# A gated unit in seven half products: first token sum, operand slots and the order of its preparation changed

## The chip, the cores and the metric

The kernel runs on one core of a Trainium2 chip. The metric is device time of one execution in microseconds. Three runs of the kernel before took 1392.05, 1392.38 and 1394.17 us; the median is 1392.38 us.

## The reference, cut to what matters

One step of a two-layer decoder for 512 prompt tokens and 8 sample tokens (520 columns here). The first layer is a state space mixer with a gated unit; the second is dilated attention. The change lies in the gated unit:

```
ga, gb = split(gelu(y) @ w_glu + b_glu, 2)   # y: 520 x 2048, w_glu: 2048 x 4096
y = ga * sigmoid(gb) * silu(z)               # 520 x 2048
out = y @ w_out                              # 2048 x 1024
```

## The kernel before, in words

Activations lie transposed: 128 features on the partitions, 520 tokens along a row. Every fp32 matrix product is made of three matmuls on rounded operands: each operand is split into a high part (rounded to fp32r on ScalarE, ACT) and a rest (operand minus high part), and the terms are high x high, high x rest, rest x high. So each weight block needs a load into `raw`, a `w_hi` on ACT and a `w_lo` on GpSimd (POOL) or VectorE (DVE) before TensorE (PE) can multiply it.

The kernel is a row of blocks of code, each with one list of instructions for each engine; at a block's border all engines wait for each other. The change touches the blocks `outputs` (it ends with the GELU), `glu` and the start of `residual` for `a_out`. The order of the work in a block is that in which each engine's function is written; engines meet through semaphores.

**The end of `outputs`.** ScalarE writes `act_hi`, VectorE `act_lo` (L1303). PE turns the last rows and then runs tile 0 of the gated unit early (`early_tile`). A tile is 128 output features over all 16 feature blocks; it has two units of 8 blocks (1024 x 128 weights), 48 matmuls each. Units 0 to 7 are the "plain" or standard units: they make output tiles 0 and 1 in the ordinary way (gb and ga of each). They use two `raw` buffers and two operand slots by turns; slot n % 2 is free for unit n when unit n-2 has been multiplied. GpSimd makes their rest (`split_lo`, L111); SP loads unit n into `raw` when the rest of unit n-2 is made.

**The groups.** The other 14 output tiles are made by seven half products each in place of eight: a 2 x 2 block scheme over halves of the features and halves of the tokens (260 columns), in the manner of Strassen and Winograd. It needs four sums of tokens (t1 to t4, each again high and rest, made once) and, in each group, four sums of weight blocks (`sum_weights(g, i)`, i = 0 to 3: gb1+gb2, that minus ga1, ga1-gb1, and ga2 minus the second; L1691 to L1697, into PSUM). Product p of a group (24 matmuls, L1542) takes raw weights for p = 0, 1, 6 (rest by GpSimd's `raw_lo`, L1488) and summed weights for p = 2 to 5 (rest by VectorE's `sum_lo`, L1703). There are three operand slots for the products; slot n % 3 (by a list) is free when product n-3 has been multiplied.

**Token sums.** t1, t2, t3 are made in nine chunks on VectorE: `first_sum` (L1668, the difference, two SBUF inputs, into PSUM), high part on ACT (L1560), then `low_sum` (L1675 to L1679, three dependent ops). They start with the block `glu`. t4 (`last_sum`, two halves c = 0, 1 of four steps each: L1470, ACT's rounding L1565, L1475, L1479, L1481) is made on GpSimd. PE waits for t1 at product 3, t2 at product 2, t3 at product 4, t4 at product 6 of the first group.

**Gates.** ACT moves each product or its running sum out of PSUM (`move_x`, L1592 to L1598) and VectorE adds and gates (L1736, `store_y` L1727). Product 2 of a group must wait for ACT's move of product 0, and this one waits until VectorE has stored all gated halves of the tile before. In the first group these are the four halves of the two standard tiles, which VectorE can make only after the last unit (`plain_gate(1)`).

**The end of `glu`.** In the last group ACT begins to round the gated y (`high(j)`, L1612 and L1614, four feature blocks a time), VectorE makes the rests (`low(j)`), and the weights of the next product, `a_out`, are rounded (L1652, L1654) and their rests made by GpSimd. PE's `early_tile` of `a_out` needs the first unit's rest, all of VectorE's moves and, block by block, the `y_lo`.

Of the kernel before, what the change touches and what calls it, by code (L numbers as in the profile page):

```python
# [24 lines left out]
P = 128  # L25
# [1064 lines left out]

def outputs(nc, mem, ten, dram):
# [27 lines left out]
    with ExitStack() as ctx:  # L1119
# [12 lines left out]
        s_free, s_out = sem("state_rows_moved"), sem("state_rows_stored")  # L1132
        mem.states_stored = s_out
# [88 lines left out]
        def _(act):  # L1222
# [44 lines left out]
            copy_state_rows(WT - 11)  # L1267
            nxt.split_hi(act, 2, 0, 1)

        @block.vector  # L1270
        def _(v):
# [42 lines left out]
            for m in range(WT - 2, WT):  # L1314
                low(m)


HALF_T = TOK // 2
PLAIN = 2
BLOCKS = ("ga1", "ga2", "gb1", "gb2")  # L1320
RAW_OF = {0: "ga1", 1: "ga2", 6: "gb2"}
SUM_OF = {2: 1, 3: 0, 4: 2, 5: 3}
Y_SUM_OF = {2: 0, 3: 1, 4: 2, 6: 3}


def glu(nc, mem, ten, dram):
# [13 lines left out]
    quarter = 8 * HALF_T * 4  # L1340
    th, tl = [], []
    for j in range(4):
        th.append(mem.at(f"y_sum_hi{j}", [P, 8, HALF_T], mem.rest + quarter * j, F32R)[0])
        tl.append(mem.at(f"y_sum_lo{j}", [P, 8, HALF_T], mem.rest + quarter * (4 + j), F32R)[0])
    t_last, _ = mem.at("y_sum3", [P, 8, HALF_T], mem.rest + quarter * 7)
# [4 lines left out]
    slots = [2, 0, 1]  # L1350
# [13 lines left out]
    chunks = [slice(0, 3), slice(3, 6), slice(6, 8)]  # L1364

    b11, b12 = ([x[:, 0:8, half] for x in (act_h, act_l)] for half in (lo_half, hi_half))
    b21, b22 = ([x[:, 8:16, half] for x in (act_h, act_l)] for half in (lo_half, hi_half))
    t1, t2, t3, t4 = ([th[j][:, :, :], tl[j][:, :, :]] for j in (1, 0, 2, 3))

    y_sums = ((b12, b11, t1), (b22, t1, t2), (b22, b12, t3))  # L1370
# [20 lines left out]
    def chunk_in_psum(q):  # L1391
        k = chunks[q % 3]
        n = (k.stop - k.start) * HALF_T
        return mem.pair[q % 2][:, 0:n].rearrange("p (k m) -> p k m", m=HALF_T)

# [3 lines left out]
    with ExitStack() as ctx:  # L1399
# [3 lines left out]
        dn = mem.glu  # L1403
        w_out = blocks(ten["a_w_out"][0, :, :])
        mem.a_out = nxt = Dense(nc, mem, "a_out", 2, [w_out[:, 8 * n:8 * n + 8, 0:P] for n in range(2)], (1, 0))
# [4 lines left out]
        y_sum, y_sum_hi, y_sum_lo = sem("y_summed"), sem("y_sum_hi"), sem("y_sum_lo")  # L1410
# [52 lines left out]
        def _(pool):  # L1463
# [19 lines left out]

            def raw_lo(n):
# [6 lines left out]
            for n in range(3, 6):  # L1491
                dn.split_lo(pool, n, n % 2)
# [58 lines left out]
        def _(act):  # L1551
# [67 lines left out]
            for q in range(3):  # L1619
                sum_hi(q)  # L1620
# [1314 lines left out]
```

## Time and profile before

| what | us |
|---|---|
| median of three runs | 1392.38 |
| the profiled execution | 1394.99 |
| its span | 1392.9 |
| PE busy in the span | 1281.4 (92%) |
| DVE / ACT / POOL busy | 885.2 / 548.2 / 487.5 |

PE is busy 92% of the span. Times in the trace count from the span's start. The block `glu` begins at 420.2 us; its products run from about 463.7 to 758 us; `a_out` begins at 761.08 us. PE here is the matmul engine; a matmul of 260 columns at full clock is issued every 0.12 us and shown with 0.28 us, since they are pipelined. A row of a timeline shows an instruction's start and duration and, in brackets, how long its engine had been idle and who released it. An instruction that has been issued but is held (by a port, for instance) shows as a longer duration and not as idle time.

### The profile page before, as it was taken

To read this page: it belongs to the slowest core of one execution; us is meant where nothing else is said; L and a number is where in the kernel's file an instruction comes from. 1 tells how busy PE (TensorE), PEld (TensorE's weight loads), DVE (VectorE), ACT (ScalarE), POOL (GpSimd) and SP (SyncE) were. 2 spreads that over 40 slices of the span, in tenths; PEclk is the share of its full clock that TensorE was granted. 3 is DMA by queue.
4 is the path that set the end of the run, shared out by engine and by line. 5 is a ranking of instruction groups with operands and counts; after the bars stand their busy time and mean duration, and the time that the engine had idled before them with its cause. 6 is when DMAs were issued, how large, how long until landed. Compare 5 with 4: busy or idle time off the path is not lost. (4 is left out here: it accounts for less than half of the span.)

```text
span 1392.9 us, 28135 instructions
## 1 busy us (share of the span) xinstructions
PE 1281.4 (92%) x11445; PEld 1200.3 (86%) x11445; DVE 885.2 (64%) x1341; ACT 548.2 (39%) x933; POOL 487.5 (35%) x286
## 2 busy tenths in 40 slices
PE   4998979989888899999998998799999999898997
PEld 4898879989888899999998997699988888788785
DVE  5886678987728877777778101773247777666532
ACT  4233342225443344444445212333355455443431
POOL 2212210000024834324434333043357767575400
PEclk9999999999999999999999999899999999999999
DMA  8468884448635234434432224135265886676501
GB/s 201 90 128 129 142 140 117 139 149 288 236 78 143 79 98 122 136 87 120 137 98 74 80 77 120 32 90 163 79 198 159 260 261 211 210 261 179 215 20 43
DMA packets 248063, 194.58 MB, mean 140 GB/s; under 512 B 44752, under 2 KB 232040, under 8 KB 247184
## 3 DMA queue, kind: packets, MB, share of 16 engines
q1 hardware_dynamic: 247152, 159.48, 43.7%
q10 hardware_dynamic: 800, 33.53, 6.8%
q8 instruction: 80, 1.31, 0.4%
q14 instruction: 31, 0.25, 0.1%
HBM read 172.60 MB, written 53.87 MB: 163 GB/s over the span
## 5 line engine op out<-in xcount | busy, mean ns | idle before, releaser
L111 POOL TENSOR_TENSOR w_lo<-raw,w_hi 128x1024 fp32r<-128x1024 f32 x89 | 215.3, 2421 | 533.6 <-ACT w_hi L106 285.7
L169 PE MATMUL acc<-act_hi,w_hi 128*128 128x256 f32 x832 | 173.7, 291 | 11.8 <-POOL w_lo L111 6.7
L169 PE MATMUL acc<-act_lo,w_hi 128*128 128x256 f32 x832 | 171.3, 288 | 0.0
L169 PE MATMUL acc<-act_hi,w_lo 128*128 128x256 f32 x832 | 170.3, 287 | 0.0
L106 ACT ACTIVATE w_hi<-raw 128x1024 fp32r<-128x1024 f32 x93 | 98.4, 1058 | 151.8 <-PE acc L169 106.0
L169 PEld LDWEIGHTS acc<-act_hi,w_hi 128*128 128x128 f32 x832 | 132.1, 193 | 14.6 <-issue 8.8
L169 PEld LDWEIGHTS acc<-act_lo,w_hi 128*128 128x128 f32 x832 | 132.7, 193 | 0.0
L169 PEld LDWEIGHTS acc<-act_hi,w_lo 128*128 128x128 f32 x832 | 132.4, 193 | 0.0
L2447 PE MATMUL acc<-act_hi,w_hi 128*128 128x256 f32 (+1 forms) x512 | 111.3, 299 | 12.3 <-ACTq L2767 11.8
L1488 POOL TENSOR_TENSOR w_lo<-raw,w_hi 128x1024 fp32r<-128x1024 f32 x28 | 78.3, 2806 | 113.1 <-ACT w_hi L1581 113.1
L2447 PE MATMUL acc<-act_lo,w_hi 128*128 128x256 f32 (+1 forms) x512 | 103.7, 284 | 0.0
L2447 PE MATMUL acc<-act_hi,w_lo 128*128 128x256 f32 (+1 forms) x512 | 103.6, 284 | 0.0
L2447 PEld LDWEIGHTS acc<-act_hi,w_hi 128*128 128x128 f32 x512 | 79.3, 191 | 19.8 <-ACTq L2767 15.6
L1542 PE MATMUL acc<-y_sum_hi,w_hi 128*128 128x260 f32 x296 | 84.6, 286 | 3.4 <-ACT gate_a L1592 2.1
L1542 PE MATMUL acc<-y_sum_hi,w_lo 128*128 128x260 f32 x296 | 84.3, 285 | 0.0
L1542 PE MATMUL acc<-y_sum_lo,w_hi 128*128 128x260 f32 x296 | 84.0, 284 | 0.0
L2282 POOL TENSOR_SCALAR scores<-scores,prob_scale 128x384 f32<-128x384 f32 x64 | 80.5, 1258 | 6.3
L2447 PEld LDWEIGHTS acc<-act_hi,w_lo 128*128 128x128 f32 x512 | 80.1, 190 | 0.0
L2447 PEld LDWEIGHTS acc<-act_lo,w_hi 128*128 128x128 f32 x512 | 80.0, 190 | 0.0
L2564 DVE SCALAR_TENSOR_TENSOR scores<-near_distances,neg_slopes,acc 128x256 f32<-128x256 f32 x64 | 30.2, 472 | 75.1 <-PE acc L2341 75.1
L1542 PE MATMUL acc<-act_hi,w_hi 128*128 128x260 f32 x224 | 63.9, 285 | 2.9 <-DVE w_lo L1703 2.2
L1703 DVE TENSOR_TENSOR w_lo<-aux,w_hi 128x1024 fp32r<-128x1024 f32 x37 | 45.2, 1222 | 33.6 <-ACT w_hi L1581 33.6
(388 smaller groups left out, 3333.9 us busy)
## 6 DMA issues: line engine op xcount, KB each, us to landing
raw<-a_w_glu SPq DMA_DIRECT2D x64, 512.0 KB, 4.5
s_kv<-cache_kv ACTq DMA_DIRECT2D x8, 4088.0 KB, 15.6
raw<-a_w_in SPq DMA_DIRECT2D x32, 512.0 KB, 4.4
raw<-b_w_in SPq DMA_DIRECT2D x32, 512.0 KB, 4.3
q_spread<-scratch_q SPq DMA_DIRECT2D x16, 768.0 KB, 7.1
raw<-a_w_out SPq DMA_DIRECT2D x16, 512.0 KB, 3.8
raw<-w_kv SPq DMA_DIRECT2D x16, 512.0 KB, 4.1
k_rows<-cache_kv SPq DMA_DIRECT2D x32, 256.0 KB, 5.7
```

The lines of the kernel that those rows point to most:

```text
L106: act.activation(self.wh[s][:, :, :], self.mem.raw[s][:, :, :], ACT.Copy).then_inc(self.hi_ready, 1)
L111: pool.tensor_tensor(self.wl[s][:, :, :], self.mem.raw[s][:, :, :], self.wh[s][:, :, :].bitcast(F32), ALU.subtract).then_inc(self.lo_ready, 1)
L169: ins = nc.tensor.matmul(mem.acc[a][:, 256 + lo:256 + hi], w[s][:, k, :], x[:, k0 + k, lo:hi], start=first and k == 0 and i == 0, stop=las ...
L1488: pool.tensor_tensor(wl[s][:, :, :], raw[block_at(g, RAW_OF[p])][:, :, :], wh[s][:, :, :].bitcast(F32), ALU.subtract).then_inc(w_lo, 1)
L1542: ins = nc.tensor.matmul(bank_of(g, p), a[s][:, k, :], x[:, k, :], start=first and k == 0 and i == 0, stop=k == 7 and i == 2, skip_group_c ...
L1703: v.tensor_tensor(wl[s][:, :, :], e_bank[SUM_OF[p] % 2], wh[s][:, :, :].bitcast(F32), ALU.subtract).then_inc(w_lo_v, 1)
L2282: pool.tensor_scalar(x[:, 0:3, :], x[:, 0:3, :], linv[:, i:i + 1], None, ALU.mult).then_inc(scaled, 1)
L2447: ins = nc.tensor.matmul(acc[a][:, 256 + lo:256 + hi], w[t % 2][:, k, :], x[:, k, lo:hi], start=k == 0 and i == 0, stop=k == 7 and i == 2)
L2564: v.scalar_tensor_tensor(x[:, 0:2, :].rearrange("p a k -> p (a k)"), near[:, r, :], slope[:, head:head + 1], src[:, 0:256], ALU.mult, ALU. ...
```

## The change

- The code of the token sums t1 to t3 goes into a class `HalfSums`, made in `outputs`. The three chunks of t1 are now made at the end of `outputs` (VectorE after the last `act_lo`, ACT around the rounding of unit 2); chunks 3 to 8 stay in `glu`.
- Standard units take their slots from `plain_slot`: unit 5 uses the third slot, which only the products used so far, and waits for nothing but its load; units 6 and 7 wait for units 3 and 4 and no longer for 4 and 5. ACT's copies of token sums are put between them in another order.
- Product slots are [2, 1, 0] in place of [2, 0, 1]. The slots of the following products `a_out` and `proj` are (0, 1) in place of (1, 0).
- GpSimd makes `raw_lo(0)` after the first half of t4, no longer before unit 6's rest. ACT rounds the second half of t4 before its loop, no longer in it after the first product's move.
- VectorE makes the fourth weight sum (i = 3) directly behind the third, one product earlier.
- At the end, `high(j)` and `low(j)` come one product later; the first weights of `a_out` are rounded one product earlier, and only after product N-3.
- In the mixer four addresses of buffers are changed.

```diff
+            half.high(act, 0)
+            half.high(act, 1)
             nxt.split_hi(act, 2, 0, 1)
+            half.high(act, 2)
...
+            v.wait_ge(lo_r, WT + 2)
+            half.first(v, 0)
+            for q in range(3):
+                if q < 2:
+                    half.first(v, q + 1)
+                half.low(v, q)
...
-    slots = [2, 0, 1]
+    slots = [2, 1, 0]
+    plain_slot = {2: 0, 3: 1, 4: 0, 5: 2, 6: 1, 7: 0}
...
-            for n in range(3, 6):
-                dn.split_lo(pool, n, n % 2)
-            raw_lo(0)
-            dn.split_lo(pool, 6, 0)
+            for n in range(3, 7):
+                plain_lo(n)
             last_sum(0, 0)
-            dn.split_lo(pool, 7, 1)
+            plain_lo(7)
             for step in range(1, 4):
                 last_sum(0, step)
+            raw_lo(0)
             raw_lo(1)
...
+            def plain_hi(n):
+                act.wait_ge(dn.landed[n % 2], 16 * (n // 2 + 1))
+                if n != 5:
+                    act.wait_ge(dn.unit_read, {3: 4, 4: 5, 6: 6, 7: 7}[n])
+                act.activation(wh[plain_slot[n]][:, :, :], raw[n % 2][:, :, :], ACT.Copy).then_inc(dn.hi_ready, 1)
...
+            plain_hi(3)
+            half_sums.high(act, 3)
+            half_sums.high(act, 4)
             plain_sigmoid(0, ga)
+            plain_hi(4)
+            half_sums.high(act, 5)
+            plain_hi(5)
+            half_sums.high(act, 6)
+            plain_hi(6)
+            half_sums.high(act, 7)
+            plain_hi(7)
+            last_sum_hi(0)
+            half_sums.high(act, 8)
             weights_hi(0)
             plain_sigmoid(1, gb)
             weights_hi(1)
             weights_hi(2)
+            last_sum_hi(1)
             for n in range(N):
...
-                if n == 0:
-                    last_sum_hi(1)
                 if p == 5:
                     sigmoid(g)
-                j = n - N + 5
+                if n == N - 3:
+                    act.wait_ge(nxt.landed[0], 16)
+                    act.wait_ge(multiplied, n + 1)
+                    act.activation(nxt.wh[0][:, :, :], mem.raw[0][:, :, :], ACT.Copy).then_inc(nxt.hi_ready, 1)
+                j = n - N + 4
                 if 0 <= j < 3:
-                    act.wait_ge(multiplied, n + 1)
+                    act.wait_ge(multiplied, n + 1 - (j == 2))
                     high(j, 4 * j, 4 * j + 4)
...
-                for i in {0: (0,), 1: (1,), 3: (2,), 4: (3,)}.get(p, ()):
+                for i in {0: (0,), 1: (1,), 3: (2, 3)}.get(p, ()):
                     if i == 2:
                         v.wait_ge(w_lo_v, 4 * g + 2)
-                    if i == 3:
-                        v.wait_ge(w_lo_v, 4 * g + 3)
...
-                j = n - N + 4
+                j = n - N + 3
                 if 0 <= j < 3:
                     low(j, 4 * j, 4 * j + 4)
```

## Rows read from the trace of the kernel before

**Rows 1.** Windows view of the whole core: busy time, count, clock, DMA share, GB/s.

```profile
426.00:437.00 11.00, 11.00 (x93) 10.94 (x92) 10.68 (x13) 2.97 (x4) 2.39 (x1) 1.00 1.11 282
436.00:456.00 20.00, 15.20 (x99) 14.82 (x99) 19.52 (x17) 8.44 (x10) 12.81 (x6) 0.83 0.23 64
468.00:488.00 20.00, 16.97 (x126) 16.44 (x125) 14.95 (x15) 8.04 (x11) 14.23 (x6) 0.91 0.36 100
488.00:508.00 20.00, 19.94 (x168) 19.77 (x167) 14.78 (x15) 8.56 (x13) 7.90 (x4) 1.00 0.41 115
756.00:776.00 20.00, 16.58 (x124) 16.23 (x123) 13.67 (x13) 7.51 (x9) 8.02 (x4) 0.91 0.19 53
```

**Rows 2.** Timeline of PE: start, duration, instruction, [idle before it <- releaser].

```profile
420.41 0.48 PE L169 MATMUL acc<-act_hi,w_hi 128*128 128x256 f32 x2 [0.47 <-PEq L1119]
...
432.05 0.48 PE L169 MATMUL acc<-act_hi,w_hi 128*128 128x256 f32 x2
...
440.66 0.51 PE L169 MATMUL acc<-act_hi,w_hi 128*128 128x256 f32 x2 [2.61 <-POOL w_lo L111]
...
450.41 0.48 PE L169 MATMUL acc<-act_hi,w_hi 128*128 128x256 f32 x2 [2.19 <-POOL w_lo L111]
...
467.06 0.36 PE L1542 MATMUL acc<-act_hi,w_hi 128*128 128x260 f32 x1 [0.50 <-POOL w_lo L1488]
...
472.25 0.48 PE L1542 MATMUL acc<-y_sum_hi,w_hi 128*128 128x260 f32 x1 [2.07 <-ACT gate_a L1592]
...
483.84 0.35 PE L1542 MATMUL acc<-act_hi,w_hi 128*128 128x260 f32 x1 [0.62 <-DVE w_lo L1703]
...
568.89 0.28 PE L1542 MATMUL acc<-y_sum_hi,w_hi 128*128 128x260 f32 x1
...
571.76 0.28 PE L1542 MATMUL acc<-act_hi,w_hi 128*128 128x260 f32 x1
```

**Rows 3.** View of line L1542: idle time before it, by releaser (us, times).

```profile
  DVE w_lo L1703: 2.6, 7
...
  DVE w_sum_lo L1703: 1.0, 3
```

**Rows 4.** Timeline of DVE (VectorE), columns as in rows 2.

```profile
420.26 1.86 DVE L1668 TENSOR_TENSOR aux<-act_hi 128x780 f32<-128x780 f32 x2 [13.87 <-PEq L1119]
...
428.76 0.98 DVE L1677 TENSOR_TENSOR aux<-aux,act_lo 128x780 f32<-128x780 f32 x1
...
466.63 3.13 DVE L1727 TENSOR_TENSOR y_gated<-gate_a,z_in 128x260 f32<-128x260 f32 x2
...
474.42 3.17 DVE L1695 TENSOR_TENSOR aux<-raw,raw 128x1024 f32<-128x1024 f32 x1
...
478.75 1.23 DVE L1703 TENSOR_TENSOR w_lo<-aux,w_hi 128x1024 fp32r<-128x1024 f32 x1 [0.83 <-ACT w_hi L1581]
...
562.13 1.23 DVE L1697 SCALAR_TENSOR_TENSOR aux<-aux,raw 128x1024 f32<-128x1024 f32 x1
```

**Rows 5.** Timelines of POOL (GpSimd) and of ACT (ScalarE), first group.

```profile
466.88 2.60 POOL L1470 TENSOR_TENSOR y_sum<-act_hi,y_sum_hi 128x1040 f32<-128x1040 f32 x1
474.10 2.41 POOL L1475 TENSOR_TENSOR y_sum<-y_sum,y_sum_hi 128x1040 f32<-128x1040 f32 x1 [4.62 <-ACT y_sum_hi L1565]
...
472.95 1.07 ACT L1565 ACTIVATE y_sum_hi<-y_sum 128x1040 fp32r<-128x1040 f32 x1
```

**Rows 6.** Timelines of PE, DVE, POOL and ACT at the stage's end.

```profile
755.16 0.36 PE L1542 MATMUL acc<-y_sum_hi,w_hi 128*128 128x260 f32 x1 [1.01 <-POOL w_lo L1488]
...
761.08 0.48 PE L169 MATMUL acc<-y_hi,w_hi 128*128 128x256 f32 x2 [2.79 <-issue]
...
751.53 4.59 DVE L1762 TENSOR_TENSOR y_lo<-y_gated,y_hi 128x1040 fp32r<-128x1040 f32 x2 [0.29 <-ACT y_hi L1612]
...
758.03 5.49 POOL L111 TENSOR_TENSOR w_lo<-raw,w_hi 128x1024 fp32r<-128x1024 f32 x2 [3.01 <-ACT w_hi L1652]
...
749.48 2.02 ACT L1612 ACTIVATE y_hi<-y_gated 128x1040 fp32r<-128x1040 f32 x2
```

More of the change, by code:

```diff
@@ L1132, in outputs @@
         s_free, s_out = sem("state_rows_moved"), sem("state_rows_stored")
+        half = mem.half_sums = HalfSums(nc, mem)
         mem.states_stored = s_out
@@ L1315, in _ @@
                 low(m)
[L1318 to L1323, printed above, removed]
+            v.wait_ge(lo_r, WT + 2)
[4 more added lines that the diff above has]
+                half.low(v, q)
 def glu(nc, mem, ten, dram):
@@ L1339, in glu @@
     mem.glu_end = o
[L1340 to L1345, printed above, removed]
+    half_sums = mem.half_sums
+    th, tl = half_sums.th, half_sums.tl
+    t_last, _ = mem.at("y_sum3", [P, 8, HALF_T], mem.rest + 7 * 8 * HALF_T * 4)
     y_dead = [mem.at(f"y_gated{n}", [P, WT, TOK], at)[0] for n, at in enumerate((mem.acth_at, mem.actl_at))]
@@ L1363, in glu @@
     lo_half, hi_half = slice(0, HALF_T), slice(HALF_T, TOK)
[L1364 to L1370, printed above, removed]
+    b11, b21, b22 = half_sums.b11, half_sums.b21, half_sums.b22
+    t1, t2, t3, t4 = half_sums.t1, half_sums.t2, half_sums.t3, half_sums.t4
     moving = (b11, b21, t2, t1, t3, b22, t4)
@@ L1389, in glu @@
     e_bank = [x[:, :].rearrange("p (k m) -> p k m", k=8) for x in mem.pair]
[L1391 to L1394, printed above, removed]
     def bank_of(g, p):
@@ L1403, in glu @@
         dn = mem.glu
+        dn.wh.append(wh2)
+        dn.wl.append(wl2)
         w_out = blocks(ten["a_w_out"][0, :, :])
-        mem.a_out = nxt = Dense(nc, mem, "a_out", 2, [w_out[:, 8 * n:8 * n + 8, 0:P] for n in range(2)], (1, 0))
+        mem.a_out = nxt = Dense(nc, mem, "a_out", 2, [w_out[:, 8 * n:8 * n + 8, 0:P] for n in range(2)])
         z_in = [sem("z_in0"), sem("z_in1")]
@@ L1510, in _ @@
             for m in range(1, 2 * PLAIN):
-                dn.tile(pe, m, m % 2, m // 2, act_h, act_l)
+                pe.wait_ge(dn.acc_free[m % 2], m // 2 + 1)
+                for u in range(2):
+                    dn.multiply(pe, 2 * m + u, plain_slot[2 * m + u], m % 2, act_h, act_l, 8 * u, u == 0, u == 1)
             for n in range(N):
@@ L1767, in low @@
                 ins.then_inc(lo_r, 1)
-            first_sum(0)
-            for q in range(9):
+            half_sums.first(v, 3)
+            for q in range(3, 9):
                 if q < 8:
-                    first_sum(q + 1)
-                low_sum(q)
-                if q == 2:
+                    half_sums.first(v, q + 1)
+                half_sums.low(v, q)
+                if q == 5:
                     plain_gate(0, ga)
@@ L1939, in ssm_out @@
     wk = blocks(ten["w_kv"])
-    mem.proj = Dense(nc, mem, "proj", 1, [wk[:, :, cols(n)] for n in range(2)], (1, 0))
+    mem.proj = Dense(nc, mem, "proj", 1, [wk[:, :, cols(n)] for n in range(2)])
     residual(nc, mem, "a_out", mem.a_out, ten["a_w_out"][0, :, :], 2, mem.yh, mem.yl, V_APOST, mem.acth_at, mem.glu_end,
```

103 lines of the change are left out of this document (60 added, 43 removed).

## The prediction

> **What bounds the kernel now.** TensorE does, in nearly the whole gated stage. I read the windows view first: in 488 to 508 us PE is busy 19.94 of 20 us at full clock, but only 15.20, 16.97 and 16.58 us in three other windows of 20 us, with a mean clock of 0.83, 0.91 and 0.91 [rows 1]. So what can be won is idle time of PE plus the slow clock behind it. PE's timeline then names the waits [rows 2, 6]. Standard units ("plain"; 5.82 us each, from 11.64 us between 420.41 and 432.05) wait 2.61 us before 440.66 and 2.19 us before 450.41, for GpSimd's rounding rest `w_lo`. Product 1 of the first group waits 0.50 us. Product 2 waits 2.07 us for ScalarE's first move of `gate_a`. At the end there are 1.01 us before the last product and 2.79 us before `a_out`. The lost clock is 20 x 0.17 = 3.4 us in 436 to 456, 20 x 0.09 = 1.8 us in 468 to 488, and 1.8 us in 756 to 776 [rows 1]. The waits of 2.61, 2.19, 2.07 and 2.79 us were each followed by such a fall from 2.4 to 1.2 GHz; that of 1.01 us was not. Last, the view of the product line: ten waits for the weight sums' `w_lo` on VectorE, 3.6 us [rows 3]. A product lasts 2.87 us (568.89 to 571.76) [rows 2].
>
> **Part 1: the first token sum, moved forward.** VectorE starts it at 420.26 now, after 13.87 us idle [rows 4]. It is three chunks: a first difference (0.93 us), then three ops of 0.98 us, smaller for the last chunk. In front of the block border, it can start when the last `act_lo` is there, about 406.4, is held by GpSimd's second rounding to about 408.6, and needs 0.93 + 0.93 + 3.0 + 0.7 + 3.0 + 2.2 = 10.8 us: done at 419.4. PE's early tile holds the border until 419.9, so the cost is 0, with 0.5 us of cover; past that, each us of delay costs one. ScalarE's three copies (0.8 us) stand around a rounding that waits for PE anyway.
>
> **Part 2: the third slot for unit 5.** Its high part needs no freed slot, so it runs once it has landed, about 428.5 (an estimate: six transfers of 512 KB fill 426 to 437, unit 5's first and unit 6's last). GpSimd has its rest by 433.2, and PE wants it at 437.9. Units 6 and 7 also ask one unit earlier than they did. What is late next is the transfer of unit 6: the DMA engines are saturated in 426 to 437 (share 1.11, 282 GB/s) [rows 1], so it lands near 436.7 (437.5 would still leave 2 us). Its rest is ready at 440.6, and PE wants it at 443.7. Unit 7: ready 445.4, wanted 449.5. So both waits and the slow clock behind them go, and the six units end at 420.41 + 6 x 5.82 = 455.3.
>
> **Part 3: product 0 gets a wait.** On GpSimd `raw_lo(0)` now stands behind the whole first half of the fourth sum. Queued in order: unit 6's rest to 440.6, `last_sum(0,0)` to 443.0, unit 7's rest to 445.4, then three steps and `raw_lo(0)`, 2.41 us each [rows 5]. VectorE's first weight sum (1.2 us) cuts in once: 445.5 + 4 x 2.45 + 1.2 = 456.5. Product 0 starts there, 1.2 us after the units. Before, it started near 463.7 (467.06 less 0.50 and 2.87).
>
> **Part 4: product 2.** It needs ScalarE's move, which needs four gated halves from VectorE. The halves start at 456.1, after the last unit. The trace shows VectorE ops with two SBUF inputs and GpSimd ops taking turns, whole ops at a time: two halves of 0.35 us took 3.13 us at 466.63, around GpSimd's op at 466.88 [rows 4, 5]. So: half 1 at 456.5, `raw_lo(1)` 456.8 to 459.2, half 2 to 459.6, `last_sum(1,0)` to 462.0, halves 3 and 4 to 462.7. ScalarE now has the 1.07 us rounding of the fourth sum [rows 5] in front of the move: 462.0 + 1.07 + 0.48 = 463.6. Product 2 could start at 462.4 (456.6 + 2 x 2.87 + issue), so PE waits 1.3 us instead of 0.50 + 2.07. That is 463.7 against 472.25: 8.5 us earlier. The slow clock behind it goes too (1.6 us): product 3 starts 10.1 us earlier, at 466.6.
>
> **Part 5: product 4 of the first group is what is late next.** Before, none of the long waits stood there, since VectorE was ahead of a PE that had waited at product 2. Now GpSimd's steps of `last_sum(1)` begin at 463.2 and no longer at 474.10 [rows 5]. VectorE has the rest of product 3's weights at 465.7 and asks for the sum `ga1 - gb1` (two SBUF inputs; 3.17 us at 474.42, against 1.23 alone) [rows 4] 0.1 us after GpSimd's next step took its turn. It runs 468.1 to 469.3. Then, new in this place, the sum with `ga2` (1.23 us), a move (0.4) and the rest (1.23): 472.1. Product 4 could have begun at 469.5, so PE waits 2.8 us, and as after the like waits above loses 1.6 us of clock. Product 5 then starts at 476.7 against 483.84 [rows 2]: **7.1 us earlier**. The bounds: GpSimd's turn missed, no wait worth naming, 11 us earlier; slow clock after the waits of 1.2 and 1.3 us as well, 4 us earlier.
>
> The Trainium skill ("SBUF — State Buffer", summary of rules for kernel authors) says that a VectorE op with two SBUF inputs and a GpSimd op that reads SBUF exclude each other, and that the second to issue fully blocks. It speaks against moving GpSimd's sum earlier. The rows agree and add the turns. A sum without that exclusion would be that of rival B below.
>
> **Part 6: the fourth weight sum, one step earlier in each group.** Now `ga2 + ...` is at 562.13 behind the rest for product 4 [rows 4], and product 5 waits 0.3 us for what follows. The shortest waits aren't listed everywhere, since ten stand in the view for 14 groups [rows 3], but groups follow each other evenly; so I take 0.32 us in each of groups 2 to 13: 12 x 0.32 = **3.8 us** (lower bound: the listed 3.6 us less about 1.0 in the first group, 2.6; upper 4.5). What pays is the rest for product 4: 1.23 us later on VectorE, less the move's overlap. From the halves' end of a group I get: move and rounding 1.5, rest 1.3, sum 1.24, sum 1.23, move 0.4, rest 1.2 = 6.9 us, and product 4 starts 7.3 us after it. So 0.4 us remain and it costs 0. The block `gb2` is asked for 2.3 us earlier, and a VectorE wait for its landing goes.
>
> **Part 7: the end.** ScalarE now rounds the last weights before the copies of `y_hi`, 2.02 us each [rows 6], so the 1.01 us before 755.16 go. The next block's first rounding moves ahead of the last products, and its rest on GpSimd (now 758.03 to 761.0, which PE's 2.79 us wait is for) asks at 752.5, beside VectorE's first `y_lo`. From product 5 on (750.8 without its wait: 755.16 less 1.01, 3.07 and 0.3), the turns are: half 1 751.9 to 753.1, GpSimd to 755.5, half 2 to 756.6 (as the 4.59 us at 751.53 now [rows 6]), move to 757.0. PE can start `a_out` at 757.2 instead of 761.08. But `y_lo` of blocks 4 to 7 comes after the gate and shares turns with the second rest: 757.9 to 759.1, GpSimd to 761.5, to 762.6. PE reaches block 4 at 760.1: a wait of 2.6 us inside the tile, and 1.6 us of clock. End of the tile 773.2 instead of 774.4 (761.08 + 96 x 0.12 + 1.8 of clock): **1.2 us** (0 if the gate is blocked once more; 3 if the clock stays).
>
> Slots (1,0) to (0,1) and the mixer's changed addresses: the same slot is free at the same unit, cost 0, hidden by waits for PE. Behind the stage all is tied to PE and to transfers that start after it, so the gain is kept.
>
> **Sum.** 7.1 + 3.8 + 1.2 = 12.1 us. The profiled execution took 1394.99 us (span 1392.9 and 2.1 around it), so it would take 1382.9. The median of the runs is 2.6 us lower, 1392.38; on that, 1380.3.
>
> **Rivals.**
> A. The forecast, 1380.3 (own range 1377.5 to 1383.5). Chance 0.50.
> B. Turns fall well: no wait at product 4 and none inside the tile. 11 + 3.8 + 2.9 = 17.7 at most, 16 likely: 1376.4. For it: the turn at 465.7 is missed by 0.1 us only. Against: both engines count from the same event. Chance 0.25.
> C. More of the front's gain is eaten: unit 6 lands late, or GpSimd's longer queue brings product 0 a 3 us wait with slow clock. 7.1 falls to 2 to 4; total 6 to 8: 1385.4. For it: the DMA is full and GpSimd has no gap from 438 to 459. Chance 0.17.
> D. Slower: the rest for product 4 becomes late in every group. One mechanism: the sum `ga1 - gb1` meets a GpSimd op each time (2.4 us), so product 4 waits 2.4 - 0.4 = 2 us, 14 times: 28 - 12 = 16 us slower, 1408. It decides from 0.4 + 12.1 / 14 = 1.3 us of delay. Against: GpSimd ends its three rests about 5 us before that sum. Chance 0.03.
> E. The waits only change place and nothing is won: 1392. For it: each wait removed has the next within 3 us. Chance 0.05.
>
> **Numbers.** Time 1380.3. The range 1374 to 1387 takes in A, nearly all of B and most of C. A measurement of this kernel tells about 0.2% (2.8 us) from no change. Faster 0.93 (A, B, C and a little of E), same 0.04, slower 0.03.
>
> **What would show it.** In the changed profile: VectorE busy from 408.6 to 419.4 and the border at 420.2 as before (part 1). No PE wait in the plain units and their end near 455.3 (part 2). A wait near 1.2 us before product 0 for GpSimd and one near 1.3 us before product 2 for ScalarE (parts 3, 4). A wait near 2.8 us before product 4 of the first group only (part 5). No waits of 0.3 us from VectorE at product 5 (part 6). No wait before the last product, PE in `a_out` about 4 us after it would be free at most, with a wait inside the tile (part 7). I am wrong if the border moves, if product 4 waits in every group, or if PE's gaps of the first group sum to over 8 us.

## The result, and the profile after

| | median us (lowest to highest) | profiled execution | ratio of the runs to before |
|---|---|---|---|
| before | 1393.27 (1392.05 to 1394.17), 4 runs | 1394.99, span 1392.9 | |
| changed | 1383.06 (1379.62 to 1384.85), 4 runs | 1379.62, span 1377.5 | 0.9924 [0.9902, 0.9947] |

That is 10.2 us less by the medians and 10.6 by the ratio; 1380.3 was forecast, 2.8 us below, with 1383.06 inside the range of 1374 to 1387. The forecast sum, 12.1 us, lies inside the ratio's interval (7.4 to 13.7 us). The profiled executions differ by 15.4 us. I split the gated block of each trace at fixed rows: from its border (the first L169 row of PE after the gap of about 0.5 us) to product 5 of the first group, then 13 groups to the last product 5, then to the border behind the first `a_out` tile. All lengths below are differences of such rows, each from one trace.

| us | whole block | border to first product 5 | 13 groups | last product 5 to border |
|---|---|---|---|---|
| before | 354.58 | 63.43 | 267.22 | 23.93 |
| changed | 339.62 | 55.55 | 261.56 | 22.51 |
| gain | 14.96 | 7.88 | 5.66 | 1.42 |

PE's timeline of the changed kernel (start, duration, instruction, [idle before it <- releaser]) answers to [rows 2, 6]:

```profile
420.28 0.48 PE L169 MATMUL acc<-act_hi,w_hi 128*128 128x256 f32 x2 [0.47 <-PEq L1184]
...
457.83 0.36 PE L1608 MATMUL acc<-act_hi,w_sum_hi 128*128 128x260 f32 x1 [2.70 <-POOL w_sum_lo L1553]
...
465.21 0.28 PE L1608 MATMUL acc<-y_sum_hi,w_hi 128*128 128x260 f32 x1
...
472.89 0.36 PE L1608 MATMUL acc<-y_sum_hi,w_hi 128*128 128x260 f32 x1 [1.79 <-DVE w_lo L1749]
...
475.83 0.29 PE L1608 MATMUL acc<-act_hi,w_hi 128*128 128x260 f32 x1
...
743.42 0.51 PE L169 MATMUL acc<-y_hi,w_hi 128*128 128x256 f32 x2
...
748.89 0.81 PE L169 MATMUL acc<-y_hi,w_hi 128*128 128x256 f32 x2 [2.34 <-DVE y_lo L1806]
...
759.90 0.48 PE L169 MATMUL acc<-y_hi,w_hi 128*128 128x256 f32 x2 [0.62 <-PEq L1456]
```

The row at 457.83 is product 0: it multiplies raw weights, and `w_sum_hi` is only the name of the third slot's buffer. The border is where it was, the units run through, and three waits are left: before product 0, before product 4 (472.89), and inside the first `a_out` tile. The windows view (length, busy time and count of PE, PEld, DVE, ACT and POOL, then clock, DMA share, GB/s) shows where clock is still lost, against [rows 1]:

```profile
436.00:456.00 20.00, 19.14 (x160) 18.93 (x158) 15.34 (x17) 7.70 (x9) 16.34 (x7) 1.00 0.30 82
456.00:476.00 20.00, 16.38 (x122) 16.23 (x123) 16.27 (x12) 5.81 (x8) 17.34 (x7) 0.91 0.22 62
488.00:508.00 20.00, 20.00 (x169) 20.00 (x169) 14.64 (x17) 8.96 (x12) 7.66 (x3) 1.00 0.42 119
744.00:764.00 20.00, 17.04 (x128) 16.65 (x127) 10.84 (x9) 4.92 (x5) 7.67 (x3) 0.91 0.23 69
```

PE's 15.20 us at clock 0.83 in 436 to 456 became 19.14 at full clock. In the view of the product line the ten waits for VectorE's rests [rows 3] are gone but for one; its whole list is

```profile
  issue: 4.8, 2
  POOL w_sum_lo L1553: 2.7, 1
  DVE w_lo L1749: 1.8, 1
```

The two "issue" entries are the weight loader's (PEld) side of the same two waits, not further ones.

The timelines of VectorE and of GpSimd tell why the three waits are there:

```profile
406.27 3.92 DVE L1135 TENSOR_TENSOR aux<-act_hi 128x780 f32<-128x780 f32 x2
...
418.23 0.70 DVE L1153 TENSOR_TENSOR y_sum_lo<-aux,act_lo 128x520 fp32r<-128x520 f32 x1
...
466.53 3.49 DVE L1741 TENSOR_TENSOR aux<-raw,raw 128x1024 f32<-128x1024 f32 x1
470.05 1.23 DVE L1743 SCALAR_TENSOR_TENSOR aux<-aux,raw 128x1024 f32<-128x1024 f32 x1
...
471.53 2.35 DVE L1749 TENSOR_TENSOR w_lo<-aux,w_hi 128x1024 fp32r<-128x1024 f32 x2
...
744.28 4.56 DVE L1806 TENSOR_TENSOR y_lo<-y_gated,y_hi 128x1040 fp32r<-128x1040 f32 x2
```

```profile
439.50 2.40 POOL L1546 TENSOR_TENSOR w_lo<-raw,w_hi 128x1024 fp32r<-128x1024 f32 x1 [6.22 <-ACT w_hi L1627]
441.86 2.90 POOL L1529 TENSOR_TENSOR y_sum<-act_hi,y_sum_hi 128x1040 f32<-128x1040 f32 x1
...
455.34 2.35 POOL L1553 TENSOR_TENSOR w_sum_lo<-raw,w_sum_hi 128x1024 fp32r<-128x1024 f32 x1
...
466.50 2.44 POOL L1538 TENSOR_TENSOR y_sum<-y_sum,act_lo 128x1040 f32<-128x1040 f32 x1
...
744.85 2.89 POOL L111 TENSOR_TENSOR w_lo<-raw,w_hi 128x1024 fp32r<-128x1024 f32 x1 [2.93 <-ACT w_hi L1720]
```

The token sum ends at 418.93, ahead of the border; in all ten traces with the sum there it ends 1.3 to 1.4 us before the border. GpSimd has no idle time from 439.50 until its rest for product 0 is done at 457.7. The sum at 466.53 takes 3.49 us because GpSimd's step of 466.50 went first; its own length is 1.23.

### The profile page after: what moved, and what is told of

Same layout as the page of the kernel before. It is cut to its first block and busy times, and to the rows that moved or that the text cites. A ratio compares the mean times of both kernels' runs of the same rounds, so it can differ in the third digit from the quotient of the medians.

```text
span 1377.5 us, 28137 instructions
## 1 busy us (share of the span) xinstructions
PE 1271.8 (92%) x11445; PEld 1194.9 (87%) x11445; DVE 874.4 (63%) x1341; ACT 547.0 (40%) x933; POOL 480.9 (35%) x286
## 5 line engine op out<-in xcount | busy, mean ns | idle before, releaser
L111 POOL TENSOR_TENSOR w_lo<-raw,w_hi 128x1024 fp32r<-128x1024 f32 x84 | 203.4, 2423 | 517.8 <-ACT w_hi L106 269.9
L169 PE MATMUL acc<-act_hi,w_hi 128*128 128x256 f32 (+1 forms) x816 | 169.3, 289 | 6.7 <-PEq L446 3.8
L169 PE MATMUL acc<-act_lo,w_hi 128*128 128x256 f32 (+1 forms) x816 | 167.0, 287 | 0.0
L169 PE MATMUL acc<-act_hi,w_lo 128*128 128x256 f32 (+1 forms) x816 | 166.3, 285 | 0.0
L106 ACT ACTIVATE w_hi<-raw 128x1024 fp32r<-128x1024 f32 x88 | 93.1, 1058 | 145.7 <-PE acc L169 108.0
L169 PEld LDWEIGHTS acc<-act_hi,w_hi 128*128 128x128 f32 x816 | 128.8, 192 | 9.1 <-issue 6.1
L169 PEld LDWEIGHTS acc<-act_lo,w_hi 128*128 128x128 f32 x816 | 129.1, 192 | 0.0
L169 PEld LDWEIGHTS acc<-act_hi,w_lo 128*128 128x128 f32 x816 | 129.0, 192 | 0.0
L2491 PE MATMUL acc<-act_hi,w_hi 128*128 128x256 f32 (+1 forms) x512 | 111.8, 300 | 12.2 <-ACTq L2811 11.7
L1553 POOL TENSOR_TENSOR w_lo<-raw,w_hi 128x1024 fp32r<-128x1024 f32 x28 | 72.3, 2590 | 112.3 <-ACT w_hi L1648 112.3
L2491 PE MATMUL acc<-act_hi,w_lo 128*128 128x256 f32 (+1 forms) x512 | 104.3, 286 | 0.0
L2491 PE MATMUL acc<-act_lo,w_hi 128*128 128x256 f32 (+1 forms) x512 | 104.3, 286 | 0.0
L2491 PEld LDWEIGHTS acc<-act_hi,w_hi 128*128 128x128 f32 x512 | 79.8, 192 | 19.7 <-ACTq L2811 15.6
L2491 PEld LDWEIGHTS acc<-act_lo,w_hi 128*128 128x128 f32 x512 | 80.5, 191 | 0.0
L2324 POOL TENSOR_TENSOR scores<-scores 128x128 f32<-128x128 f32 x64 | 38.5, 601 | 74.1 <-DVE prob_scale L2623 74.0
L1608 PE MATMUL acc<-act_lo,w_hi 128*128 128x260 f32 x224 | 63.5, 283 | 0.0
```

The source lines that it names most:

```text
L106: act.activation(self.wh[s][:, :, :], self.mem.raw[s][:, :, :], ACT.Copy).then_inc(self.hi_ready, 1)
L111: pool.tensor_tensor(self.wl[s][:, :, :], self.mem.raw[s][:, :, :], self.wh[s][:, :, :].bitcast(F32), ALU.subtract).then_inc(self.lo_ready, 1)
L169: ins = nc.tensor.matmul(mem.acc[a][:, 256 + lo:256 + hi], w[s][:, k, :], x[:, k0 + k, lo:hi], start=first and k == 0 and i == 0, stop=las ...
L1553: pool.tensor_tensor(wl[s][:, :, :], raw[block_at(g, RAW_OF[p])][:, :, :], wh[s][:, :, :].bitcast(F32), ALU.subtract).then_inc(w_lo, 1)
L1608: ins = nc.tensor.matmul(bank_of(g, p), a[s][:, k, :], x[:, k, :], start=first and k == 0 and i == 0, stop=k == 7 and i == 2, skip_group_c ...
L2324: pool.tensor_tensor(x[:, 2, :], x[:, 2, :], x[:, 3, :], ALU.add).then_inc(scaled, 1)
```

## The experiments

Theory T was that each of the three parts pays where the forecast put it: front by token sum and slot, groups by the weight sum, end by the new order. Each was undone or done alone; GpSimd's and ScalarE's new order in the front and the mixer's addresses were not, so what they bring is not shown by itself. Two parts lie too close in whole times (5 us or less) for the runs alone, so each kernel's block is compared too.

**Does the block repeat?** The changed kernel, unaltered.

> The changed kernel itself, unaltered, as the measure for the others and for a second trace. Its executions so far took 1379.6 to 1384.9 us, those of the kernel before 1392.1 to 1394.2. Theory: the spread is the slow clock behind short waits of PE (1.8 to 2.7 us long before products 0 and 4 and inside the a_out tile): an execution of about 1384 us shows one to three falls to 1.2 GHz more, 1.6 us each, and otherwise the same times. Rival: the spread lies in the mixer, in its transfers of q, and the gated stage ends at the same time in every execution. Median 1382 to 1384.

Measured: 1383.15 us (1379.3 to 1387.41), ratio 0.9899 [0.9878, 0.9919] on this chip, where before took 1397.01: 14.1 us. Block 339.51, 0.1 from the first. The profiled execution was 3.5 us longer than the first one (1383.14 against 1379.62), and none of that lies in the block: 1.3 us come before it and 2.3 behind. So the theory of more slow clock in the gated stage fell, and blocks of single traces can be compared more finely than whole times, within a limit that the second trace of the kernel before shows below. The two ratios agree where their intervals overlap, from 0.9902 to 0.9919, which of 1395 us is 11 to 14.

**The weight sum alone**, on the kernel before.

```
-                for i in {0: (0,), 1: (1,), 3: (2,), 4: (3,)}.get(p, ()):
+                for i in {0: (0,), 1: (1,), 3: (2, 3)}.get(p, ()):
...
-                    if i == 3:
-                        v.wait_ge(w_lo_v, 4 * g + 3)
```

> The kernel before with one edit: the fourth weight sum directly behind the third. Theory: PE's wait at product 5 goes in all 14 groups; groups follow each other each 20.15 us instead of 20.56, so 5.7 us less: 1387.5 (1387 to 1389). Rival: that wait only goes because the whole change puts VectorE ahead of PE, or because of other gaps; alone the edit moves the wait to product 4 (its weights' rest comes 1.2 us later): 1392 to 1394, within 0.1% of before.

**The changed kernel without it** (the same lines put back).

> The changed kernel with the fourth weight sum back in its old place. Theory: the parts add up, so it is 5.3 us slower than the changed kernel (13 groups of 0.41 us): about 1388.4. In the first group product 4's wait before (1.8 us, behind the GpSimd turn) gets 1.2 us shorter. Rival: the old place costs nothing once the rest is changed: 1383.

| | us | ratio | block | front | 13 groups | end |
|---|---|---|---|---|---|---|
| weight sum alone | 1382.68 | 0.9909 [0.9888, 0.9930] | 344.34 | 62.97 | 261.56 | 19.81 |
| changed, without it | 1390.57 | 0.9952 [0.9936, 0.9968] | 345.84 | 55.78 | 266.41 | 23.65 |

The weight sum alone brings 5.66 us in 13 groups against the first trace of before and 4.93 against the second (267.22 and 266.49); in the changed kernel taking it back costs 4.85. That is 0.37 to 0.44 us a group. With the early sum every group takes 20.12 us; with the late one they take 20.38 to 20.67, unevenly, in all three traces. At the end it brings 4.1 us more against the first trace (2.6 against the second), if the old end is kept. The run's theory had only the groups (5.7 us) and missed this; its rival, that the wait moves to product 4, is excluded by the 20.12 us. This one edit is worth 10.2 us of block; all else without it is worth 8.7, and both together 15.0 and not 19.0. Most of the overlap, 3.0 of 4.0 us, is at the end. (Against the second trace of before: 8.0, 6.5, and 12.7 for 14.5.) Taking the sum back cost 6.2 us of block where 5.3 were expected; product 4's wait in the first group fell to 1.41 us, and one of 0.60 came back at product 5. PE's timeline of the weight sum alone:

```profile
440.69 0.51 PE L169 MATMUL acc<-act_hi,w_hi 128*128 128x256 f32 x2 [2.61 <-POOL w_lo L111]
...
752.39 0.48 PE L169 MATMUL acc<-y_hi,w_hi 128*128 128x256 f32 x2 [1.51 <-issue]
...
764.77 0.48 PE L169 MATMUL acc<-y_hi,w_hi 128*128 128x256 f32 x2 [0.62 <-PEq L1399]
```

Its tile has 752.39 to 764.15 (764.77 less 0.62), 11.76 us, at full clock after a wait of 1.51. Before, the tile took 13.29 us, 1.53 of them clock, after 2.79 us of wait, with 1.01 us in front of the last product. The wait in front of the last product is gone too, without the new end. ScalarE's timelines say what was late: the rounding of the last weight sum, which the copies of `y_hi` are queued behind. First before:

```profile
748.55 1.03 ACT L1581 ACTIVATE w_sum_hi<-aux 128x1024 fp32r<-128x1024 f32 x1 [2.25 <-DVE aux L1697]
```

and with the weight sum early:

```profile
739.84 1.03 ACT L1581 ACTIVATE w_sum_hi<-aux 128x1024 fp32r<-128x1024 f32 x1
740.75 2.03 ACT L1612 ACTIVATE y_hi<-y_gated 128x1040 fp32r<-128x1040 f32 x2
```

ScalarE's idle time of 2.25 us is gone, and with it most of what PE waited for at `a_out`.

**The old end in the changed kernel.**

```
-                if n == N - 3:
...
-                    act.activation(nxt.wh[0][:, :, :], mem.raw[0][:, :, :], ACT.Copy).then_inc(nxt.hi_ready, 1)
-                j = n - N + 4
+                j = n - N + 5
...
+                if n == N - 2:
+                    act.wait_ge(nxt.landed[0], 16)
+                    act.activation(nxt.wh[0][:, :, :], mem.raw[0][:, :, :], ACT.Copy).then_inc(nxt.hi_ready, 1)
...
-                j = n - N + 3
+                j = n - N + 4
```

> The changed kernel with the old order at the end of the gated block (copies and rests of the gated y one product earlier, first a_out weights rounded after them). Lengths count from border to border of the gated block: 354.6 us in the kernel before, 339.6 in the changed one, 344.3 with the weight sum alone. Theory: the new end is a loss once the weight sum is earlier; with the old end the last part (from the last product 5 to the border) takes 19.8 us as with the weight sum alone and not 22.5, since PE no longer stops inside the a_out tile and its clock stays: 336.9, so 2.7 us faster than the changed kernel. Rival: the end gains what was forecast (1.2 us), so the old end makes it slower: 341 or more.

Measured: 1380.84 us, 0.9892 [0.9872, 0.9913]; block 336.69, end 19.83. The changed kernel's new end takes 22.60 and 22.51. So beside the early weight sum the new end costs 2.7 us: with it PE begins `a_out` at once (743.42) but waits 2.34 us inside the tile and loses 15.86 - 11.76 - 2.34 = 1.76 us of clock (743.42 to 759.28 is 15.86), 4.1 in all, against a wait of 1.5:

```profile
747.94 0.48 PE L169 MATMUL acc<-y_hi,w_hi 128*128 128x256 f32 x2 [1.52 <-issue]
```

Part of the 2.7 us is the clock fall, which not every execution has: the kernel that gives VectorE its turn (below) has the same end with a wait of 2.32 us and no fall, and takes 21.25, still 1.4 us more. In whole times the difference (0.9892 against 0.9899 and 0.9924) can't be told apart.

**The token sum back in its old place.**

```
-            half.high(act, 0)
...
-            half.first(v, 0)
-            for q in range(3):
...
-                half.low(v, q)
...
-            half_sums.first(v, 3)
-            for q in range(3, 9):
+            half_sums.first(v, 0)
+            for q in range(9):
...
-                if q == 5:
+                if q == 2:
                     plain_gate(0, ga)
```

> The changed kernel with the three chunks of the first token sum back at the start of the gated block (and the first gate of a standard tile behind chunk 2 again). Theory: VectorE has 10.8 us more to do before the first weight sums and only 3.3 us of slack there, so the gated halves, ScalarE's move and product 2 come 5 to 7 us later: 1388 to 1390. Rival: the front is bound by GpSimd's chain up to the rest for product 0, VectorE's time there is free, and moving the token sum brought at most 2 us: 1383 to 1385.

Measured: 1388.59 us, 0.9933 [0.9915, 0.9951]; front 61.15 against 55.38, the rest equal (261.53, 22.64). ScalarE's copies of the token sums stand in an order of their own in this run. PE's timeline has a wait in the units, now before unit 7 (units 5 and 6 run through), and a long one at product 0:

```profile
455.30 0.81 PE L169 MATMUL acc<-act_hi,w_hi 128*128 128x256 f32 x2 [2.45 <-POOL w_lo L1537]
...
466.54 0.56 PE L1599 MATMUL acc<-act_hi,w_sum_hi 128*128 128x260 f32 x1 [3.90 <-POOL w_sum_lo L1544]
```

```profile
450.00:470.00 20.00, 13.66 (x88) 13.27 (x87) 19.66 (x17) 6.95 (x8) 19.84 (x8) 0.79 0.10 29
```

In this window (columns as above) VectorE is busy 19.66 of 20 us and GpSimd 19.84, waits for turns included: the two engines, not PE, are full. The time came as the theory had it, but not its path through the gated halves and product 2: GpSimd's first step of the fourth token sum waits for VectorE's token sum, and all of GpSimd's queue up to the rest for product 0 comes later:

```profile
449.71 3.23 POOL L1520 TENSOR_TENSOR y_sum<-act_hi,y_sum_hi 128x1040 f32<-128x1040 f32 x1 [3.00 <-DVE y_sum_lo L1153]
```

Of the front's 7.9 us, 5.6 to 5.8 come from the token sum leaving this stretch. The other 2.3 (63.43 less 61.15) come from the rest of the change there and are not taken apart.

**Without the third slot** (the slots in two turns as before, each rounding waiting for its unit; the slots of the next products and the mixer's addresses go back too).

```
-    slots = [2, 1, 0]
-    plain_slot = {2: 0, 3: 1, 4: 0, 5: 2, 6: 1, 7: 0}
+    slots = [2, 0, 1]
+    plain_slot = {2: 0, 3: 1, 4: 0, 5: 1, 6: 0, 7: 1}
...
-                if n != 5:
-                    act.wait_ge(dn.unit_read, {3: 4, 4: 5, 6: 6, 7: 7}[n])
+                act.wait_ge(dn.unit_read, n + 1)
```

> The changed kernel with the standard units in two slots by turns again (unit n waits until unit n-2 has been multiplied), all else as changed. Theory A, from the changed trace: unit 5's rounding then waits for unit 3 (432) instead of its landing (429), its rest is ready at 435.5 and wanted at 437.8; unit 6 waits for its landing (438.4) either way; unit 7's rest moves by under 1 us, wanted 449.4. So the third slot brings nothing: the gated block takes 339.6 within 0.7. Rival, as forecast: the third slot is what removed the 2.6 and 2.2 us waits before units 5 and 6 with the slow clock behind them, so without it the block takes 343 to 347.

Measured: 1385.26 us, 0.9924 [0.9903, 0.9946]; block 339.60, front 55.63. With the rest of the change in place the third slot brings nothing. ScalarE's timeline without it:

```profile
436.69 1.06 ACT L1626 ACTIVATE w_hi<-raw 128x1024 fp32r<-128x1024 f32 x1 [4.25 <-DMA raw<-a_w_glu]
...
442.20 1.06 ACT L1626 ACTIVATE w_hi<-raw 128x1024 fp32r<-128x1024 f32 x1 [3.75 <-PE acc L169]
```

One rounding waits for its transfer, as in the changed kernel ([3.40 <-DMA] at 438.37), the next for PE, and PE waits for neither. What made the 2.61 us wait in the kernel before shows in its own ScalarE timeline: unit 5's slot was free at 432.05, but its rounding stood behind two copies of token sums, and the second waited for VectorE:

```profile
436.41 0.82 ACT L1560 ACTIVATE y_sum_hi<-aux 128x780 fp32r<-128x780 f32 x1 [2.81 <-DVE aux L1668]
437.13 1.05 ACT L106 ACTIVATE w_hi<-raw 128x1024 fp32r<-128x1024 f32 x1
```

Without the slot, but in ScalarE's new order, that rounding starts when PE frees its slot (at 430.67 in that trace, 11.9 us behind the border; 16.7 before). With the token sum back but the slot kept (the run before this one), it starts 11.2 us behind the border, behind one copy and not two, so there the slot can have given 0.4 us. That leaves ScalarE's order as the likely reason; undoing it alone was not tried.

**Giving VectorE its turn at product 4.** In the first group GpSimd's second step waits until the sum `ga1 - gb1` is done.

```
             for step in range(4):
+                if step == 1:
+                    pool.wait_ge(summed, 3)
                 last_sum(1, step)
```

> The changed kernel, with GpSimd's second step of the second half of the fourth token sum held until VectorE has made the weight sum ga1 - gb1 of the first group. Theory: product 4 of that group waits 1.8 us only because that sum lost its turn to GpSimd (it shows as 3.49 instead of 1.23 us); with the turn the wait goes or falls under 0.5, and product 6 waits 0.5 to 1 us for the token sum instead: the block is 338.3 to 339.6. Rival: product 4 waits for the longer chain on VectorE itself (the fourth weight sum is in front of its weights' rest), so at least 1.2 us of the wait stay.

Measured: 1384.46 us, 0.9928 [0.9899, 0.9956]; block 339.73. The mechanism is right: VectorE's sum takes 1.23 us and the wait before product 4 is gone. But the delayed steps end later, PE waits 1.93 us at product 6 (0.5 to 1 expected), and its clock falls there:

```profile
465.96 1.23 DVE L1743 TENSOR_TENSOR aux<-raw,raw 128x1024 f32<-128x1024 f32 x1
```

```profile
478.20 0.36 PE L1610 MATMUL acc<-y_sum_hi,w_sum_hi 128*128 128x260 f32 x1 [1.93 <-POOL w_sum_lo L1553]
```

```profile
476.00:496.00 20.00, 18.07 (x139) 17.89 (x138) 13.22 (x14) 7.65 (x10) 7.57 (x4) 0.91 0.30 83
```

Up to the second product 5 this kernel takes 77.04 us from the border, the changed one 75.67. The 2.35 us gained up to the first product 5 (53.20 for 55.55) are more than lost behind it (3.72: the wait of 1.93 and 1.8 of clock); the end, in this one execution, took 21.25 for 22.51 and hides it.

**The front in another order.** GpSimd makes the rest for product 0 before the second step of the fourth token sum and that for product 1 before the third, for which it also waits until four gated halves are stored. VectorE stores the four halves before the rest of product 2's weights, and ScalarE's rounding of the second half comes after product 1. The end is the old one.

```
-            for step in range(1, 4):
-                last_sum(0, step)
             raw_lo(0)
+            last_sum(0, 1)
             raw_lo(1)
+            pool.wait_ge(gated, 4)
+            for step in range(2, 4):
+                last_sum(0, step)
```

> e4_old_end with the first group's order changed: VectorE gates tile 0 before the last unit is done, GpSimd makes the rests for products 0 and 1 ahead of the steps of the fourth token sum and starts the later steps only when all four gated halves are stored; ScalarE's second rounding of that sum comes after product 1. Theory: the waits of 2.7 us before product 0 (with a clock fall) and of 1.8 us before product 4 come from GpSimd's queue and turns; they go, and one of 2 to 3 us comes before product 6, for the fourth token sum. Front part (border to first product 5) 50 to 52 instead of 55.5, whole block 335 instead of 336.9 of e4. Rival: GpSimd's total work bounds the front, so product 6 waits for all of it: no difference to e4, 337 to 338.

**The same, with an end of its own:** the first `a_out` rounding ahead of the third copy, and VectorE's rests for blocks 4 to 11 ahead of the last gate.

```
+                for j in {N - 4: (0,), N - 2: (1, 2)}.get(n, ()):
+                    low(j, 4 * j, 4 * j + 4)
                 if p == 5:
```

> e6_gates_first with another end: the first a_out weights are rounded after product N-3 and before the third copy of the gated y, and VectorE makes the rests of blocks 4 to 11 before the last gate. Theory: the first rest of a_out is ready when PE is done with the products (the 1.5 us wait goes), and no block of y is late by more than 0.5 us: the last part takes 18 us instead of 19.8, the block 333.2. Rival: GpSimd's and VectorE's turns only change place, a block of y is late by 2 us inside the tile with a clock fall, and the last part takes 21 or more.

**The same without GpSimd's pause.**

```
-            pool.wait_ge(gated, 4)
...
-                if n == 1:
+                if n == 0:
                     last_sum_hi(1)
```

> e7_new_end without GpSimd's pause: it goes on with the steps of the fourth token sum without waiting for the four gated halves, and ScalarE rounds its second half after product 0. Theory: the 4.6 us wait before product 6 in e6 and e7 was GpSimd's sum starting late; now it is done 3 us earlier, paid with up to 2.5 us before product 2 by turns with VectorE. Border to second product 5: 73.5 (76.9 with the pause, 75.4 in the changed kernel); the block 333.5. Rival: whatever the order, GpSimd's work sets when product 6 can start, 76 to 77, block 336 to 337.

**The changed kernel's front with that end.**

> e4_old_end (front as changed) with the end of e7_new_end. Theory: the parts are independent, so the block takes 55.4 + 261.6 + 18.5 = 335.5 us. Rival: the end depends on what the front leaves (transfers of the a_out weights, turns), and takes 19.8 as in e4.

| | us | ratio | block | border to second product 5 | end |
|---|---|---|---|---|---|
| changed | 1383.06, 1383.15 | 0.9924, 0.9899 | 339.62 | 75.67 | 22.51 |
| gates first | 1379.93 | 0.9883 [0.9860, 0.9907] | 338.29 | 76.93 | 19.92 |
| and own end | 1377.51 | 0.9871 [0.9846, 0.9897] | 336.93 | 76.93 | 18.56 |
| and no pause | 1374.75 | 0.9863 [0.9832, 0.9894] | 332.84 | 72.82 | 18.58 |
| changed front, own end | 1377.82 | 0.9890 [0.9860, 0.9920] | 335.46 | 75.46 | 18.56 |

The end of its own gives 1.3 to 1.4 us more than the old end (18.56 for 19.83 and 19.92), and the last row's block is what adding up the parts had given (335.5). The front in the new order with the pause was expected at 50 to 52 us to the first product 5 and took 49.95, but the block took 338.29 for 335: the pause made a longer wait than it removed, at product 6 (76.93 for 75.42 with the old order), as the rival had it:

```profile
480.48 0.56 PE L1610 MATMUL acc<-y_sum_hi,w_sum_hi 128*128 128x260 f32 x1 [4.58 <-POOL w_sum_lo L1553]
```

Without the pause, PE waits twice and keeps its clock, and both lengths come within 0.7 us of the expected ones (72.82 for 73.5, 332.84 for 333.5):

```profile
465.16 0.36 PE L1609 MATMUL acc<-y_sum_hi,w_hi 128*128 128x260 f32 x1 [1.33 <-DVE w_lo L1751]
...
478.75 0.36 PE L1609 MATMUL acc<-y_sum_hi,w_sum_hi 128*128 128x260 f32 x1 [1.87 <-POOL w_sum_lo L1553]
```

```profile
456.00:476.00 20.00, 18.67 (x156) 18.49 (x155) 17.06 (x15) 8.21 (x10) 18.58 (x8) 1.00 0.32 92
476.00:496.00 20.00, 18.13 (x152) 17.96 (x151) 13.56 (x15) 7.63 (x10) 9.14 (x4) 1.00 0.34 99
```

This is the fastest kernel of the study: 19 us below before by the ratio, and its interval lies below that of the first comparison of the changed kernel (from 0.9902) and of the kernel with its turn given, run on the same chip (from 0.9899). It overlaps the changed kernel's second one. Its block is 6.8 us shorter than the changed kernel's.

**How well does the block before repeat?** The kernel before, unaltered.

> The kernel before itself, as a null measure and for a second trace of it. Theory: the three parts of the gated block repeat to 0.2 us (63.4, 267.2, 23.9 from border to border: 354.6), as those of the changed kernel did (339.6 and 339.5), and what differs between executions lies before and behind that block. Rival: the block itself varies by some us in the kernel before, so that the difference of 15.0 us between two traces overstates the change. Ratio 1.000 within 0.003.

Measured: ratio 0.9985 [0.9961, 1.0009]; block 352.35: front 63.46 and groups 266.49 (0.0 and 0.7 from the first), end 22.40 for 23.93. The theory of 0.2 us fell for the end and for the groups. At the end PE waited as long as in the first trace, but its clock did not fall behind it:

```profile
760.79 0.48 PE L169 MATMUL acc<-y_hi,w_hi 128*128 128x256 f32 x2 [2.78 <-issue]
```

```profile
756.00:776.00 20.00, 16.60 (x137) 16.24 (x135) 13.39 (x12) 7.11 (x9) 10.31 (x4) 1.00 0.26 77
```

The equal fronts hide another fall. Before unit 6 PE waited 2.19 us in the first trace and its clock fell, 2.17 in the second and it did not (clock 0.83 and 0.91 in 436 to 456). PE then stood waiting for GpSimd's rest at product 1 the longer, 2.05 us for 0.50, and the product began 46.7 us behind the border in both:

```profile
467.50 0.36 PE L1542 MATMUL acc<-act_hi,w_hi 128*128 128x260 f32 x1 [2.05 <-POOL w_lo L1488]
```

So that fall, about 1.6 of the 3.4 us of slow clock that the prediction counts there, cost nothing. Against this block the changed one gains 12.7 us and not 15.0, and only the front's 7.9 are the same in both comparisons.

## Why the forecast was right, and where it was not

The forecast sum was 12.1 us; the block gained 15.0 against one trace of before and 12.7 against the other, while the runs give 10.6 and 14.1. Case A holds, in part by luck: the front's waits and slow clock were forecast at 6.9 us in sum (1.2, 1.3, 2.8 and 1.6) and came to 6.1 (2.70, 1.79 and 1.6), in other places; the groups gave more than the upper bound; and the new end, counted at 1.2 us, gains 0.3 with the late weight sum and costs 1.4 to 2.7 with the early one.

- **Part 1, right.** The chain ended at 418.93 (419.4 forecast), the border did not move. The forecast gave it a cost of 0 and no worth of its own; taken back alone it costs 5.8 us of front.
- **Part 2, right in the times, wrong in the cause.** Both waits and the slow clock are gone, and the units end at 457.83 - 2.70 = 455.1 (455.3 forecast). But without the slot the block is equal (339.60). The step that failed is "its high part needs no freed slot" as the reason: before, unit 5's rounding was late (437.13) by the copies of token sums in ScalarE's queue and not by its slot (free at 432.05). Nor was all of the slow clock there to be won, as the second trace of before shows.
- **Part 3, right place, too small.** The wait before product 0 was 2.70 us for 1.2. GpSimd's steps that read while VectorE reads took 2.90 us (and 3.29 for a later one), where the sum put 2.41 and one cut of 1.2; unit 6 landed 1.7 us later than estimated (438.37 for 436.7). And the clock fell here: most of product 0 ran at 0.42 us for an instruction of 0.28, and it took 4.49 us (457.83 to 462.32) for 2.87.
- **Part 4, wrong as a wait.** ScalarE's move came as forecast (463.79 for 463.1), but PE, slowed, came after it: product 2 at 465.21 (463.7 forecast) waits for nothing, product 3 follows at 468.07 for 466.6.
- **Part 5, right.** GpSimd took the turn (466.50, VectorE 466.53 with 3.49 us; the order and the wait, 1.8 us, are the same in four more traces with this front and weight sum), and product 4 waited 1.79 us for 2.8, since PE came later. The clock was lost at product 0 and not here. Product 5 is at 475.83 for 476.7, 8.0 us earlier where 7.1 were forecast. The kernel that gives VectorE the turn shows that rival B's gain in the front was not to be had by that turn: the next wait, of 1.93 us, stands two products later. Its other half, an end without a wait in the tile, was to be had by another order (18.56 for 22.51).
- **Part 6, right mechanism, mis-sized.** 0.37 to 0.44 us a group in 13 groups, 4.9 to 5.7 us, where 0.32 x 12 = 3.8 was taken from the listed waits, with 4.5 as upper bound. The groups are not even (20.38 to 20.67 us), but their mean was there to be read: before, product 5 to product 5 took 267.22 / 13 = 20.56 us (20.50 in the second trace), and 7 products of 2.87 are 20.09. The difference, 0.47, is within 0.04 of the gain against the same trace.
- **Part 7, right in size, wrong in the cause.** The end gained 1.4 us for 1.2, with the wait inside the tile at 2.34 for 2.6 and the clock fall behind it. But against the second trace of before (22.40, without a fall) it gained nothing. And what it gained is not the new order's: with the weight sum late the new end takes 23.65 us for 23.93, both with a fall. What the forecast missed is that part 6 already brings the end from 23.93 to 19.81, the 1.01 us before the last product included, because ScalarE's copies no longer stand behind a late rounding. Beside it the new end loses 2.7 us (1.4 without a fall).
- Rival C's mechanism (unit 6 late, a 3 us wait at product 0 with slow clock) did come about (a wait of 2.70 us); it cost less, since what was forecast behind product 0 shrank by more: 1.3 us at product 2, 1.0 at product 4 and its 1.6 of clock. Rival D did not show: no wait stands at product 4 after the first group.

## What to carry to other kernels

A stage of equal groups has its gain in the distance between equal products, less the products' own time; the list of waits showed only part of it here. When several edits touch one engine's queue, undo each alone: here beside the smallest edit another (the new end) did harm, and a third (the slot) did nothing, while the sum of all looked right. When two engines take turns, moving a wait by ordering them anew pays only where the later one has slack, so look for the product behind the one that is mended. And slow clock in front of a wait for another engine costs nothing: look where the wait ends before counting it.

## What the runs showed of the hardware

**A wait of PE of 2 to 3 us costs clock in one execution and not in another.** Before `a_out`, 2.79 us were followed by clock 0.91 in the window [rows 1, 6], and 2.78 us in another execution by 1.00. Before unit 6, 2.19 us were followed by a fall and 2.17 us in the other execution were not. Inside the tile, 2.34 us in the changed kernel were followed by 0.91, 2.32 us in the kernel with its turn given by 1.00:

```profile
740.00:760.00 20.00, 16.96 (x135) 16.21 (x135) 17.55 (x13) 9.24 (x11) 8.33 (x3) 1.00 0.18 53
```

Waits of 1.33 and 1.87 us in one kernel were not followed by a fall, one of 1.93 in another was. A fall cost PE 1.5 to 1.8 us (1.53 before, 1.62 at product 0 and 1.76 in the tile of the changed kernel). So a block's length has a part of this size, for each such wait with nothing later to hide it, that one trace doesn't settle. It explains 1.5 of the 2.2 us between the two blocks of before; the other 0.7 lie in the groups.

**VectorE and GpSimd take turns op by op**, also where VectorE has several ops queued: the pairs at 738.42 and 744.28 of the changed kernel took 4.61 and 4.56 us beside GpSimd's ops at 739.00 and 744.85, where two ops alone take about 2.5 (an estimate from 1.23 us for a sum of 128x1024). The Trainium skill ("SBUF — State Buffer", summary of rules for kernel authors) says that the second to issue fully blocks. The rows agree for one op (3.49 us for 1.23) and the pairs fit a pair that is split by the other engine's next op.

**A stage without waits repeats, a whole run does not.** The 13 groups took 261.53 to 261.56 us in seven executions of kernels whose groups have the same code and no wait. Where short waits stand in each group they did not repeat so well: 267.22 and 266.49 us in two traces of the kernel before. Whole runs of one kernel spread over 4 to 11 us. Over the fourteen traces the block's border lies at 418.5 to 423.6 us and the stretch behind the block takes 615.4 to 623.3, so the spread arises on both sides of it. What makes it stays open, and so does why some waits cost clock and others not.
